# One or two products of the next weight job are put behind TensorE's own last work of five stages

## The chip, the cores and the metric

The kernel runs on one core of a Trainium2 chip. The metric is device time in microseconds (us) of one execution, lower is better. TensorE multiplies, ScalarE evaluates activations and copies, VectorE does elementwise work, GpSimd helps with memsets, some products and the gathers of cache pages, and SyncE issues most transfers.

## The reference

Two layers of a hybrid decoder trunk are computed for a prompt group (512 tokens) and a sample group (8 sequences of 4 tokens). A layer projects the normed input with one wide matrix, runs four mixers side by side, gates and sums their projected outputs, and ends with a gated feed-forward:

```python
h = rmsnorm(x, lp['norm1'])
(a_q, a_k, a_v, a_iq, a_ik, a_iw, r_q, r_k, r_v, r_g,
 c_q, c_f, c_i, c_g, m_z, m_xbc, m_dt, gates) = jnp.split(h @ lp['w_in'], SPLIT_POINTS, axis=-1)
...
o_a = attention_prompt(q, iq, iw, k, v, a_ik)          # A: top-k sparse attention
o_b, ret_new = retention_mixer(r_q, r_k, r_v, r_g, pos, states[0])     # B: retention
o_c, hgrn_new = hgrn2_mixer(c_q, c_f, c_i, c_g, lp['lb'], lp['hgrn_norm'], states[1])  # C: HGRN2
o_d, ssm_new, conv_new = mamba2_mixer(m_z, m_xbc, m_dt, ...)           # D: Mamba-2 with a causal conv
branches = jnp.stack([o_a, o_b, o_c, o_d], axis=2)
up = jnp.einsum('btnw,nwd->btnd', branches, lp['w_branch'])
g = jax.nn.sigmoid(gates.reshape(B, T, N_BRANCH, D_MODEL))
x = x + jnp.sum(g * up, axis=2) @ lp['w_out']
ff_gate, ff_up = jnp.split(rmsnorm(x, lp['norm2']) @ lp['w_gu'], 2, axis=-1)
x = x + (jax.nn.silu(ff_gate) * ff_up) @ lp['w_down']
```

All is float32. Both groups share the weights, so their 544 token columns go through every projection together.

## The kernel before

**Jobs and products.** The weights of a layer stream through two slots of the buffer `ring`, one job (512 columns of a weight matrix) in each. The jobs are `aq`, `akv`, `iq`, `ikiw`, `r0` to `r2`, `c2`, `r3`, `c0`, `c3`, `z`, `c1`, `xbc0`, `xbc1`, `dt`, then the gates and the branch projections in the order `gate00`, `gate01`, `wb00`, `gate10`, `wb01`, `gate11`, `wb10`, `gate20`, `wb11`, `gate21`, `wb20`, `gate30`, `wb21`, `gate31`, `wb30`, `wb31`, and last the jobs of the feed-forward. A job up to `wb31` is cut into products, the rows of the list `table`: a "natural" job has five (four token tiles of 128 and one of 32, at lines 369 and 372), a gate, `iq`, `c0` or `xbc` job eight (four strips of 128 output columns by two halves of 272 tokens, line 378), each of 8 matmuls, and a `wb` job eight of 4 matmuls. One matmul of a full product is called a unit here; the trace shows every float32 matmul as two records. `wb01#7` is the seventh product of `wb01`.

**Banks.** A product adds up in a bank of PSUM, `bank_of[k]`, mostly 6 or 7, in some stages one of three. Before its first matmul TensorE waits until the bank's last user has been read. Products of gate and projection jobs are read by ScalarE (`take_act`: a copy or an activation, and for the projections a transfer to DRAM), those of `wb` jobs by VectorE (`take_dve`: two instructions, lines 488 and 490, or one, line 485). The last product of a gate job is released only after a sigmoid over the whole gate. The first product of a gate job also waits in ScalarE's queue until VectorE has read the last `wb` product that used the same gate buffer.

**Stages and points.** The mixers run stage by stage, each written by hand for all engines: the end of stage A's projections (share `r0`), prompt attention (`c2`), sample attention (`dt`), retention (`wb01`), HGRN2 (`wb11`), the causal conv (`wb20`), the state space part (`gate31`), then the feed-forward. Between the mixer's own instructions stand points, at which a class `Share` fills products in: it spreads the units from where the last share ended to the end of the job it is named after over the points by a list of weights, so `Share("wb20", [4] + [1] * 8)` does four twelfths of its units at the first point. TensorE's `point` issues units up to its place, and the takers' `point` at the same index reads the products up to the one before the product that is under way there (`fill_to`):

```python
k = max(i for i in range(len(table)) if starts[i] < max(upto, 1))
take_to(who, eng, k - 1)
```

`share.end` finishes the job on each engine.

**Joins.** Each stage is a block that all five engines enter and leave together. Some stages are also a `part` of their own, behind which SyncE clears the stage's semaphores in a further block: so behind `wb01` and `wb11`, but not behind `r0`, `c2` and `wb20`. TensorE can't start the next stage before the last engine has left the one before.

In the conv stage TensorE first fills in products (the point with the weight 4), then turns the conv state (line 2055), ScalarE copies that (line 2029), and only then VectorE starts its convolutions (from line 2001), a sequence that goes on to the end of the stage, with `wb20`'s products read in between. Behind `share.end` TensorE makes short sums and transposes (lines 2064 to 2072) and ScalarE copies them out (lines 2046 and 2047). The top-k searches of the attention are long sequences on VectorE (lines 949 and 950), and the weights 1, 18, 25, 34 in the share `c2` are the units put beside them.

Of the kernel before, what the change touches and what calls it, by code (L numbers as in the profile page):

```python
# [133 lines left out]
def trunk(nc, inp, out):  # L134

    es = ExitStack()
    with es:
# [68 lines left out]
        class Arena:  # L206
            def __init__(self, t, at=0, end=None):
                self.t, self.at, self.end = t, at, end
# [103 lines left out]
        END = {}  # L312
# [14 lines left out]
            spare[name] = (2, 6, 7)  # L327
        bank_of, bank_before, last_use = [], [], [-1] * 8
        for k, row in enumerate(table):
            b = min(spare.get(row[0], (6, 7)), key=lambda i: last_use[i])  # L330
            bank_of.append(b)
            bank_before.append(last_use[b])
            last_use[b] = k
        starts = [0]
# [161 lines left out]
        def fill_to(who, eng, upto):  # L496

            if who == "pe":
                for x in range(done["pe"], upto):
                    k = max(i for i in range(len(table)) if starts[i] <= x)  # L500
                    product(eng, k, x - starts[k])
                done["pe"] = max(done["pe"], upto)
                return
            k = max(i for i in range(len(table)) if starts[i] < max(upto, 1))
            take_to(who, eng, k - 1)

        def take_to(who, eng, upto):
            for k in range(done[who], upto):
                if who == "act" and table[k][0][:4] == "gate" and table[k][5] == "act":

                    last = [i for i in range(k) if table[i][5] == "dve" and
                            table[i][0][3:] == table[k][0][5:]]
                    if last:
                        eng.wait_ge(S("taken_dve"), taken_by(last[-1])[1])
                (take_act if who == "act" else take_dve)(eng, k)
            done[who] = max(done[who], upto)

        def finish_to(who, eng, name):

            if who == "pe":  # L520
                fill_to("pe", eng, starts[END[name]])
            else:
                take_to(who, eng, END[name])

        class Share:

            def __init__(self, last, weights):
                self.a = {w: starts_at[0] for w in ("pe", "act", "dve")}
                self.a0, self.b = starts_at[0], starts[END[last]]
                self.cum = np.cumsum(weights) / np.sum(weights)  # L530
                self.p = {"pe": 0, "act": 0, "dve": 0}
                self.last = last
                starts_at[0] = self.b

            def point(self, who, eng):
                x = self.a0 + int(round((self.b - self.a0) * self.cum[self.p[who]]))
# [3 lines left out]
            def end(self, who, eng):  # L540
                assert self.p[who] in (0, len(self.cum)) or who == "dve", (who, self.p[who], len(self.cum))
                finish_to(who, eng, self.last)
        starts_at = [0]


# [116 lines left out]
        def stage_a(l):  # L662
# [48 lines left out]
            done["dve"] = END["ikiw"]  # L711
            starts_at[0] = starts[END["ikiw"]]

            share = Share("r0", [6, 12] + [1.2] * 10)
            with nc.Block() as block:
                @block.vector
                def _(dve):
# [83 lines left out]
            weights = []  # L801
            for i in range(NT):
                weights += [1] * 8 + [(1, 18, 25, 34)[i]] + [1] * 18
            share = Share("c2", weights)
            with nc.Block() as block:
                @block.sync
                def _(sp):
# [468 lines left out]
        def stage_retention(l):  # L1276
# [17 lines left out]
            qm = brT_[:, 8 * T + 2048:8 * T + 3072].rearrange("p (b n) -> p b n", b=NB)  # L1294
            kds = kT[:, P:2 * P]
            added = (0, 1, 4, 3)
            share = Share("wb01", [6] + [1] * 25)
            job0 = J["wb01"] - 1
            with nc.Block() as block:
                @block.tensor  # L1300
# [209 lines left out]
        def stage_hgrn(l):  # L1510
# [39 lines left out]
            zsum = cst[:, C["tri"][0]:C["tri"][0] + 1024]  # L1550
            lvz = K("lv_sum").rearrange("p (l t) -> p l t", l=7)
            mask = K("lv_mask").rearrange("p (s n) -> p s n", s=6)
            share = Share("wb11", [5] + [3, 3, 4, 4, 4, 3] * 4 + [3, 3, 4, 4, 4])
            with nc.Block() as block:
                @block.gpsimd
                def _(pool):
# [412 lines left out]
        def stage_ssm(l):  # L1969
# [14 lines left out]
            acc, accs = ar.take(2, SEQ), cv.take(2, NS)  # L1984
            ut, au = ar.take(5, 8), ar.take(5, 8)
            ea = ar.take(8)
            share = Share("wb20", [4] + [1] * 8)

            with nc.Block() as block:
                @block.gpsimd  # L1990
# [730 lines left out]
```

## Time and profile before

| | |
|---|---|
| times of three runs | 3776.77, 3788.73, 3782.89 us; median 3782.89 |
| profiled execution | 3787.7 us, its span in the trace 3785.9 |
| busy in the span | TensorE 91%, VectorE 46%, ScalarE 20%, GpSimd 7% |
| mean granted TensorE clock | 0.94 |
| moved | 366.11 MB in 274973 packets |

Times in the trace count from the start of the span. PE is TensorE, PEld its weight loads, DVE VectorE, ACT ScalarE, POOL GpSimd, SP SyncE; a q behind a name is the engine's sequencer. "Idle before" is time in which an engine had nothing to do, and what ended it is its releaser. A granted clock of 1.00 is 2.4 GHz, 0.50 is 1.2 GHz. The second layer repeats the first some 1857 us later with nearly the same rows.

### The profile page before, as it was taken

How to read it: one execution, taken by the hardware profiler on the slowest of the kernel's cores; microseconds unless marked ns; L12 is line 12 of the kernel's file. 1: busy time of each engine (PE TensorE's matmuls, PEld its weight loads, DVE VectorE, ACT ScalarE, POOL GpSimd, SP SyncE). 2: the span in 40 equal slices, each digit the busy share in tenths (PEclk: the TensorE clock that was granted, in tenths of full speed). 3: DMA queues.
4: the chain of work that ended last, by engine and by line, in shares of the span. 5: the costliest groups of instructions: out<-in, count | busy, mean ns of one | idle time of the engine just before them, and what ended most of it. 6: DMA issues, size and time to landing. Idle time of an engine off the chain costs nothing. (4 is left out here: it accounts for less than half of the span.)

```text
span 3785.9 us, 45247 instructions
## 1 busy us (share of the span) xinstructions
PE 3434.0 (91%) x18070; PEld 2409.5 (64%) x18070; DVE 1754.9 (46%) x3303; ACT 739.8 (20%) x1576; POOL 265.7 (7%) x266
## 2 busy tenths in 40 slices
PE   4988899989988989999989888999989998899998
PEld 2643454667666767888846434555776676678887
DVE  2135378114545445454512562951345454554543
ACT  1122222212322211010002222221123232110000
POOL 0000221210100010000000004112001000000000
PEclk8988899979999999999999889998899999999999
DMA  3221254452313221222232103555232231322221
GB/s 122 74 77 38 71 177 158 153 172 95 101 52 127 68 93 59 75 90 72 73 96 95 40 35 125 178 171 180 94 127 81 67 109 37 115 67 89 67 81 66
DMA packets 274973, 366.11 MB, mean 97 GB/s; under 512 B 39262, under 2 KB 171230, under 8 KB 274628
## 3 DMA queue, kind: packets, MB, share of 16 engines
q1 hardware_dynamic: 232348, 260.85, 21.1%
q0 software_dynamic: 21504, 75.51, 6.1%
q10 hardware_dynamic: 20904, 26.78, 2.0%
q8 instruction: 146, 2.39, 0.3%
q14 instruction: 71, 0.58, 0.0%
HBM read 312.76 MB, written 50.34 MB: 96 GB/s over the span
## 5 line engine op out<-in xcount | busy, mean ns | idle before, releaser
L378 PE MATMUL ps<-hT,ring 128*128 128x272 f32 x3072 | 780.6, 409 | 61.8 <-PEq L155 32.3
L378 PEld LDWEIGHTS ps<-hT,ring 128*128 128x128 f32 x3072 | 593.1, 198 | 213.7 <-issue 56.5
L372 PE MATMUL ps<-ring,hT 128*128 128x512 f32 (+3 forms) x1600 | 661.0, 555 | 34.5 <-DVE hT L625 18.3
L372 PEld LDWEIGHTS ps<-ring,hT 128*128 128x128 f32 (+1 forms) x1600 | 280.3, 199 | 327.1 <-issue 302.9
L378 PE MATMUL ps<-branchT,ring 128*128 128x272 f32 x1024 | 264.2, 412 | 38.5 <-DVE arena L488 23.7
L2511 PE MATMUL ps<-hT,ring 128*128 128x272 f32 x1136 | 279.0, 396 | 17.4 <-DVE hT L2636 17.4
L378 PEld LDWEIGHTS ps<-branchT,ring 128*128 128x128 f32 x1024 | 198.4, 198 | 97.0 <-DVE arena L488 28.6
L2511 PEld LDWEIGHTS ps<-hT,ring 128*128 128x128 f32 x1136 | 217.9, 192 | 63.6 <-issue 18.2
L2511 PE MATMUL ps<-arena,ring 128*128 128x272 f32 x720 | 177.9, 401 | 13.3 <-PEq L155 10.6
L2511 PEld LDWEIGHTS ps<-arena,ring 128*128 128x128 f32 x720 | 139.8, 195 | 44.5 <-issue 11.4
L949 DVE MAX8 branchT<-arena 32x8 f32<-32x2080 f32 x64 | 148.2, 2316 | 2.2
L950 DVE MATCH_REPLACE8 arena<-branchT,arena 32x2080 f32<-32x2080 f32 x64 | 147.0, 2296 | 0.0
L2522 ACT ACTIVATE arena<-ps 128x272 f32<-128x272 f32 x68 | 27.1, 398 | 519.7 <-PE ps L2511 519.7
L2511 PE MATMUL ps<-branchT,ring 128*128 128x272 f32 x512 | 127.1, 392 | 0.0
L2511 PE MATMUL ps<-branchT,arena 128*128 128x272 f32 x448 | 111.1, 392 | 0.0
L2511 PEld LDWEIGHTS ps<-branchT,ring 128*128 128x128 f32 x512 | 97.3, 190 | 20.1
L1188 ACT ACTIVATE branchT<-ps 128x512 f32<-128x512 f32 x128 | 69.5, 594 | 194.7 <-PE ps L1093 194.4
L721 DVE TENSOR_TENSOR branchT<-arena 128x2560 f32<-128x2560 f32 (+1 forms) x4 | 8.6, 2154 | 190.6 <-PEq L681 190.6
L2511 PEld LDWEIGHTS ps<-branchT,arena 128*128 128x128 f32 x448 | 85.1, 190 | 17.5
L2511 PE MATMUL ps<-branchT,stage 128*128 128x272 f32 x352 | 87.8, 392 | 0.0
L840 PE MATMUL ps<-cst,arena 128*128 128x128 f32 x160 | 35.4, 327 | 52.0 <-ACT arena L891 51.7
L1267 DVE TENSOR_SCALAR rows_at<-rows_at 128x32 int32<-128x32 int32 x2 | 0.4, 180 | 168.2 <-PE ps L1157 168.2
(481 smaller groups left out, 4473.4 us busy)
## 6 DMA issues: line engine op xcount, KB each, us to landing
ring<-in_w_in SPq DMA_DIRECT2D x44, 2048.0 KB, 8.1
ring<-in_w_gu SPq DMA_DIRECT2D x44, 1024.0 KB, 6.5
spill<-stage ACTq DMA_DIRECT2D x72, 256.0 KB
arena<-spill SPq DMA_DIRECT2D x16, 1024.0 KB, 5.9
ring<-in_w_branch SPq DMA_DIRECT2D x16, 1024.0 KB, 5.1
ring<-in_w_down SPq DMA_DIRECT2D x8, 1536.0 KB, 6.6
ring<-in_w_down SPq DMA_DIRECT2D x8, 1280.0 KB, 5.9
ring<-in_w_out SPq DMA_DIRECT2D x4, 2048.0 KB, 9.2
```

The source lines that it names most:

```text
L372: mm = pe.matmul(bank[0:m, 0:w], hT[:, c, t0:t0 + m], slot3(j)[:, c, 0:w], start=(c == 0), stop=(c == kn - 1))
L378: mm = pe.matmul(bank[:, 0:HALF], slot3(j)[:, c, at:at + P], src, start=(c == 0), stop=(c == kn - 1))
L721: vch.link(dve, dve.tensor_tensor(t2, a2, a2, ALU.mult))
L840: mm = pe.transpose(ps[2 + n % 2][:, s * P:s * P + P], Pr[:, n % 2, s * P:s * P + P], ident)
L949: vch.link(dve, dve.max(m, src))
L950: vch.link(dve, dve.match_replace(work, m, src, TAKEN))
L1188: act.activation(KT[:, bb, j, :], ps[j][:, :], ACT.Copy).then_inc(S("kt_ready"), 1)
L1267: vch.link(dve, dve.tensor_scalar(rows_at[:, :], rows_at[:, :], float(n_rows // DEPTH), None, ALU.add))
L2511: mm = pe.matmul(bank(n, p), left[:, c, :], r[:, c, :], start=(c == 0), stop=(c == k - 1))
L2522: act.activation(part_of[n % 2][0], bank(n, 1), ACT.Copy).then_inc(S("p1_copied"), 1)
```

## The change

A `Share` gets a third argument, `more`. Its points are spread as before up to the end of the job it is named after, but on all engines `share.end` then goes on for `more` products of the next job, and the next share starts behind these. It is 1 for `r0` (first product of `r1`) and `c2` (first of `r3`), and 2 for `wb01` (`gate11`), `wb11` (`gate21`) and `wb20` (`gate30`). The first two products of these gates are kept to banks 6 and 7.

```diff
+            early = row[0] in ("gate11", "gate21", "gate30") and row[2] == 0
-            b = min(spare.get(row[0], (6, 7)), key=lambda i: last_use[i])
+            b = min((6, 7) if early else spare.get(row[0], (6, 7)), key=lambda i: last_use[i])
...
-            def __init__(self, last, weights):
-                self.a = {w: starts_at[0] for w in ("pe", "act", "dve")}
-                self.a0, self.b = starts_at[0], starts[END[last]]
+            def __init__(self, last, weights, more=0):
+
+                self.a0, self.b, self.upto = starts_at[0], starts[END[last]], END[last] + more
...
-                starts_at[0] = self.b
+                starts_at[0] = starts[self.upto]
...
             def end(self, who, eng):
...
                 finish_to(who, eng, self.last)
+                if who == "pe":
+                    fill_to("pe", eng, starts[self.upto])
+                else:
+                    take_to(who, eng, self.upto)
...
-            share = Share("r0", [6, 12] + [1.2] * 10)
+            share = Share("r0", [6, 12] + [1.2] * 10, 1)
...
-            share = Share("c2", weights)
+            share = Share("c2", weights, 1)
...
-            share = Share("wb01", [6] + [1] * 25)
+            share = Share("wb01", [6] + [1] * 25, 2)
...
-            share = Share("wb11", [5] + [3, 3, 4, 4, 4, 3] * 4 + [3, 3, 4, 4, 4])
+            share = Share("wb11", [5] + [3, 3, 4, 4, 4, 3] * 4 + [3, 3, 4, 4, 4], 2)
...
-            share = Share("wb20", [4] + [1] * 8)
+            share = Share("wb20", [4] + [1] * 8, 2)
```

The lines below the class stand five further down in the changed kernel, so line 378 is 379 there, and line 2055 is 2060. On TensorE the end of the retention stage and the start of the HGRN2 stage (the branches are the join) read so before; `ring` stands for the streamed weights:

```order
L1360 MATMUL ps<-branchT 128x512 x4
L378 MATMUL ps<-branchT,ring 128x272 x8
L1360 MATMUL ps<-branchT 128x512 x4
L1299 UNCONDITIONAL_BRANCH
L1573 UNCONDITIONAL_BRANCH
L378 MATMUL ps<-hT,ring 128x272 x9
L1580 MATMUL ps<-cst,arena 128x128 x4
L1585 MATMUL ps<-arena,cst 128x512
```

and so with the change:

```order
L1365 MATMUL ps<-branchT 128x512 x4
L379 MATMUL ps<-branchT,ring 128x272 x8
L1365 MATMUL ps<-branchT 128x512 x4
L379 MATMUL ps<-hT,ring 128x272 x16
L1304 UNCONDITIONAL_BRANCH
L1578 UNCONDITIONAL_BRANCH
L379 MATMUL ps<-hT,ring 128x272 x8
L1585 MATMUL ps<-cst,arena 128x128 x4
L1590 MATMUL ps<-arena,cst 128x512
```

Sixteen matmuls of `gate11` stand ahead of the join, and the first point behind it has 8 in place of 9. On TensorE the conv stage reads so before (from its first row to the start of the sums behind `share.end`):

```order
L378 MATMUL ps<-hT,ring 128x272 x32
L2055 MATMUL ps<-cst,branchT 128x24 x8
L378 MATMUL ps<-hT,ring 128x272 x32
L378 MATMUL ps<-branchT,ring 128x272 x32
L2064 MATMUL ps<-arena,cst 128x8 x12
```

and so with the change:

```order
L379 MATMUL ps<-hT,ring 128x272 x27
L2060 MATMUL ps<-cst,branchT 128x24 x8
L379 MATMUL ps<-hT,ring 128x272 x21
L379 MATMUL ps<-branchT,ring 128x272 x32
L379 MATMUL ps<-hT,ring 128x272 x16
L2069 MATMUL ps<-arena,cst 128x8 x12
```

Ahead of the conv state's transposes stand 27 matmuls in place of 32, behind them 21 in place of 32, and 16 of `gate30` come in between `wb20` and the sums.

## Rows read from the trace of the kernel before

**Rows 1.** The page: busy us of the engines, with share and instructions.
```profile
PE 3434.0 (91%) x18070; PEld 2409.5 (64%) x18070; DVE 1754.9 (46%) x3303; ACT 739.8 (20%) x1576; POOL 265.7 (7%) x266
```

**Rows 2.** Windows a:b, shares c2, dt, wb11, wb20, gate31: length, busy by engine, clock.
```profile
206.85:430.48 223.63, 190.62 (x768) 92.10 (x769) 121.61 (x320) 55.05 (x147) 0.04 (x1) 0.85 0.14 49
430.48:813.38 382.90, 354.75 (x1983) 206.28 (x1983) 176.77 (x159) 88.41 (x180) 98.36 (x98) 0.91 0.49 164
...
975.78:1165.41 189.63, 169.53 (x1618) 119.09 (x1619) 96.68 (x268) 56.51 (x101) 21.10 (x20) 0.94 0.23 72
1165.41:1229.42 64.01, 54.64 (x244) 43.87 (x245) 35.73 (x87) 20.43 (x46) 0.00 (x0) 0.93 0.45 141
1229.42:1411.16 181.74, 160.14 (x822) 126.60 (x823) 86.25 (x142) 35.75 (x71) 11.26 (x8) 0.95 0.23 72
```

**Rows 3.** Timeline at the joins behind r0 and c2: start, us, engine, line.
```profile
205.25 1.10 ACTq L463 DMA_DIRECT2D spill<-stage  x1
206.85 0.46 PE L822 MATMUL ps<-arena 64*128 64x128 f32 x2 [2.54 <-PEq L715]
...
427.79 0.59 ACT L445 ACTIVATE stage<-ps 128x512 f32<-128x512 f32 x1
428.41 0.33 ACTq L463 DMA_DIRECT2D spill<-stage  x1
...
429.14 0.53 ACTq L463 DMA_DIRECT2D spill<-stage  x1
...
430.48 0.99 PE L1040 MATMUL ps<-arena,cst 32*128 32x8 f32 x4 [3.22 <-PEq L805]
```

**Rows 4.** Timeline at the joins behind wb01, wb11 and wb20.
```profile
972.97 0.78 DVE L485 TENSOR_TENSOR arena<-ps,xT 128x272 f32<-128x272 f32 x2
...
975.78 6.24 PE L378 MATMUL ps<-hT,ring 128*128 128x272 f32 x18 [5.22 <-PEq L155]
...
1161.98 0.44 DVE L490 TENSOR_TENSOR arena<-arena 128x272 f32<-128x272 f32 x1
...
1165.41 17.53 PE L378 MATMUL ps<-hT,ring 128*128 128x272 f32 x64 [4.00 <-PEq L155]
...
1229.42 1.09 PE L2160 MATMUL ps<-cst,arena 128*128 128x128 f32 x4 [3.50 <-PEq L1989]
```

**Rows 5.** Timeline: two runs of products without a wait.
```profile
368.27 20.01 PE L372 MATMUL ps<-ring,hT 128*128 128x512 f32 x46
...
1191.47 12.81 PE L378 MATMUL ps<-hT,ring 128*128 128x272 f32 x48 [4.07 <-ACT xT L416]
```

**Rows 6.** TensorE's waits: who, for whom: us in total, times, longest.
```profile
PE ps L840 <- ACT arena L891: 51.7, 10, 9.4
...
PE ps L378 <- DVE arena L488: 29.8, 14, 4.3
...
PE ps L2230 <- DVE arena L2367: 16.2, 6, 6.1
```

**Rows 7.** Timeline of the conv stage: its first step and its end.
```profile
1184.39 0.29 DVE L2001 COPY arena<-arena 128x256 f32<-128x256 f32 x1 [21.97 <-ACT arena L2029]
...
1219.20 2.10 PE L378 MATMUL ps<-branchT,ring 128*128 128x272 f32 x8 [0.60 <-DVE arena L488]
...
1221.13 2.74 PE L2064 MATMUL ps<-arena,cst 128*128 128x8 f32 x24
...
1222.03 0.44 DVE L490 TENSOR_TENSOR arena<-arena 128x272 f32<-128x272 f32 x1
```

**Rows 8.** Timeline and windows: a short wait, and the clock behind waits.
```profile
1046.65 2.85 PE L378 MATMUL ps<-branchT,ring 128*128 128x272 f32 x8 [2.03 <-ACT xT L419]
...
975.78:979.60 3.82, 3.82 (x9) 2.89 (x10) 3.58 (x3) 1.24 (x1) 3.27 (x3) 0.50 1.03 290
1047.80:1051.30 3.50, 3.50 (x8) 2.02 (x7) 2.63 (x8) 0.69 (x3) 0.00 (x0) 0.51 0.15 33
1165.41:1170.70 5.29, 5.29 (x12) 4.02 (x13) 0.00 (x0) 0.00 (x0) 0.00 (x0) 0.50 0.93 286
```

## The prediction

> **What bounds the kernel now.** I read the page first: TensorE is busy 91% of the span, VectorE 46% [rows 1]. The windows by stage say the same of each stage the change touches: in the prompt attention (`c2`) TensorE is busy 190.6 of 223.6 us against VectorE's 121.6, in HGRN2 (`wb11`) 169.5 of 189.6 against 96.7, in the conv stage (`wb20`) 54.6 of 64.0 against 35.7 [rows 2]. So a stage mostly lasts as long as TensorE's own program, and the change leaves that program's instructions alone; it moves some across five joins. Two questions remain. How much of the idle time at a join do the moved products use up? And does the next stage get shorter by all that it has lost? The timeline at the joins answers the first: TensorE stands 2.54, 3.22, 5.22, 4.00 and 3.50 us [rows 3, 4], 18.5 us in a layer, 37 us in both. The list of TensorE's waits answers the second: it also waits inside stages, for the top-k searches 51.7 us (line 840, mostly one wait in each of three query blocks), for VectorE to read `wb` products 29.8 us (line 378), and in the state space stage 16.2 us (line 2230) [rows 6]. A unit taken away in front of such a wait only makes it longer.
>
> **What a moved product costs.** 46 records of natural products took 20.01 us, 48 of gate products 12.81 us less their tail, about 0.435 and 0.235 to 0.267 a record [rows 5]. A product has 16 records: I take 7.0 us for a natural one and 3.75 us for a gate's at full speed, so 7.5 us for two. A natural unit is then 0.87 us, a gate's 0.47 us. Each layer moves 7.0, 7.0, 7.5, 7.5 and 7.5 us.
>
> **The joins and the stages behind them, one layer.** Each time: what the join comes later, then what the next stage gives back.
>
> Behind `r0`. The 2.54 us are ScalarE's: it reads the last product and issues its transfer from 205.25 to 206.35, and TensorE goes on at 206.85 [rows 3]. With `r1#1` behind it, the same follows the new last product; its bank is free, so TensorE runs on for 7.0 us. Only the transfer is shorter (that of a full tile is issued in 0.33 us, row 428.41, not in 1.10), so the join is +6.2 us. Next, share `c2` has 112 units in place of 120, by weights that sum to 182, of which 78 lie at the searches. There the stage goes by VectorE, and 3.4 of the 8 units come off the long waits [rows 6]; the other 4.6 units give 4.0 us. Together +2.2.
>
> Behind `c2`. ScalarE reads the last products of the old job only from 427.79 on [rows 3], and `r3#1` needs the bank of the first of them, so it starts 1.1 us late and ends at 435.4. Reading it (0.6) and issuing the transfer (0.33) take 1.1 with what lies between them, and leaving the block 0.8, as from 429.67 to 430.48 [rows 3]: the join comes at 437.3 in place of 430.48, +6.8. The sample attention has TensorE busy 354.8 of 382.9 us [rows 2] and gives back 8 units, 6.8 with a little lost at its gathers. Together 0.
>
> Behind `wb01`. Here VectorE is last. It ends at 973.75, TensorE at 970.56, and TensorE starts again 2.0 us after VectorE (two blocks, with the semaphores cleared between) [rows 4]. The two `gate11` products run 970.56 to 978.1; their banks are free, the second's at 973.4 when it is wanted at 974.3. ScalarE reads the last until 978.6, plus 2.0: 980.65 against 975.78, +4.9. This join hides 2.6 us. HGRN2 gives back 16 units, 7.5, less what goes into waits. One unit at its first point is lost, since TensorE waits there for VectorE's first sequence anyway, and the waits for VectorE at `wb` products eat more. Against that the products shift along the points: `wb10`, which was spread over two token tiles, falls into one, and the read of its last product, for which `gate20` waited, comes a point earlier, ahead of a long VectorE sequence; the sigmoid of `gate11` comes two points earlier, ahead of copies that TensorE needs. I take −6.1. Together −1.2.
>
> Behind `wb11`. VectorE ends at 1162.42, TensorE at 1161.41, and TensorE restarts 3.0 later [rows 4]. The two `gate21` products end at 1168.9, their read at 1169.4, the restart is at 1172.4: +7.0, so this join hides half a microsecond. The conv stage gives back little. Its length is TensorE's first point (17.53 us [rows 4]) and then VectorE's own sequence from 1184.39 to 1222.47, 38.1 us, for which TensorE waits, not the reverse: `wb20#8` starts at 1219.20, when VectorE has read `wb20#5` [rows 7]. So of 16 units only those at the first point count, 5 (27 for 32), 2.3 us. Together +4.7.
>
> Behind `wb20`. The two `gate30` products stand ahead of the sums of line 2064, which now start at 1221.13, and for which ScalarE's copies and then the join wait [rows 7]. The first needs the bank of `wb20#6`, read 2.4 us before VectorE's end (the reads follow each other at 0.95 us: `wb20#5` at 1219.15, `wb20#8` by 1222.47 [rows 7]), the second that of `wb20#8`. So they run from 2.4 us before VectorE's end to 5.1 after it, where the sums now start 1.3 before it: +6.5. The state space stage gives back 16 units, 7.5, less some 2.5 units in front of the wait of line 2230 [rows 6], plus about 1.3 us since the 4.3 us wait for VectorE meets TensorE later: −7.3. Together −0.8.
>
> The sum is 2.2 + 0 − 1.2 + 4.7 − 0.8 = +4.9 us a layer.
>
> **The clock.** Behind the `wb01` join TensorE works 3.82 us at a granted 0.50, behind `wb11` 5.29 us [rows 8], which costs 1.9 and 2.6 us. With the change the first gap shrinks from 5.22 to about 2.5. A wait of only 2.03 us was followed by 3.50 us at 0.51 [rows 8], so the half clock does not go away; I take back 1.0 us a layer, with 0 and 4.5 as ends. The Trainium skill (TensorE: Matmul & The Clock Gate, Why this matters for your kernels) advises keeping idle gaps between bursts of matmuls short, so that the clock stays up; by it the `wb01` join would be spared its half clock, 1.9 us a layer. The trace speaks against it at gaps of this length, with the 2.03 us wait.
>
> **Forecast.** 4.9 − 1.0 = +3.9 us a layer, +7.8 in all. Against the profiled execution's own 3787.7 us that is 3795.5; that execution lies 4.8 above the median, so the median becomes about **3791**, or +0.2%. Within 0.3%, 11.3 us here, a measurement of this kernel can't tell it from no change.
>
> **Ends of the terms.** The joins' +6.2, 6.8, 4.9, 7.0, 6.5 are sure to about 0.5 each. What is not known is what HGRN2 and the state space stage give back. Above, each can't give more than 7.5 plus its waits for VectorE's reads; I take 10. Below, all units could land in front of waits; I take 3. The searches could take all 8 units' worth of waiting and the clock with it: 3 us more.
>
> **Rivals.**
> *Slower: HGRN2 and the state space stage give back half.* Place: TensorE at `wb` products, where it waits for VectorE's point. VectorE gets there after a fixed sequence of its own from something TensorE made, so a thinner filling reaches the bank sooner and waits longer. For it: the fourteen waits of line 378 [rows 6]. Against it: VectorE is busy only 96.7 of 189.6 us there [rows 2]. It gives 6.7 in place of 13.4 a layer: +10.6 a layer, 3804. It decides from 1.7 us a layer missing, where the whole passes 0.3%.
> *The conv stage follows TensorE after all.* Then it gives back 7.5, not 2.3: −1.3 a layer, 3780. For it: TensorE is busy 54.6 of 64.0 us [rows 2]. Against it: VectorE's unbroken sequence behind 1184.39.
> *The clock stays up behind the joins* (the rule above). Both 1.9 and 2.6 are spared, 3.5 a layer more than I took: +0.4 a layer, 3784. The 2.03 us wait speaks against it [rows 8]. With the rival before it, −4.8 a layer: 3773, at the edge of faster.
> That the change does not do what it says is out: the order has 16 more matmuls ahead of the join.
>
> **Chances.** Forecast 0.45 (3780 to 3798), slower rival 0.30, conv rival 0.10, clock rival 0.10, both 0.05. Of the forecast's 0.45 a fifth lies past +0.3%; of the slower rival nine tenths do; of the two single ones a fifth lies past −0.3%. With half of the double one and 0.02 for what I have missed, faster is 0.04 + 0.03 + 0.02 = 0.09, slower 0.09 + 0.27 = 0.36, and same 0.55. The range reaches from the double rival to the slower one: 3774 to 3804.
>
> **What would show it.** In the profile after: gaps at the joins of about 2.3, 3.3 (in two parts), 2.5, 3.5 and 3.5 us; the conv stage's VectorE sequence still 38 us, and the stage from its first product to the next stage's first longer than 64.0 us, about 68; HGRN2 from join to join 189.6 − 6.1 + 7.0, about 190.5; the top-k waits longer by 0.7 to 1.3 us each. I am wrong if HGRN2 or the state space stage differ by over 3 us from this, or if VectorE's sequence in the conv stage stretches or shrinks. The feed-forward, 497.8 us a layer, must not change.

## The result, and the profile after

The changed kernel takes 3798.47 us (median of 11 runs) against 3785.64 for the kernel before (11 runs): ratio 1.0038, 95% interval 1.0027 to 1.0048, so +14 us and slower by a little more than the measurement's uncertainty. I had forecast 3791, in a range of 3774 to 3804, with most of the chance on "no difference". One of the 11 runs, at 4449 us, was disturbed and is left out of the ratio; the median of the other ten is 3795.6.

The profiled execution took 3792.77 us (span 3791.0), only 5 above that of before. That is chance, since layer 1 of before held the longer form of a stage that varies by itself, as the windows show. First the page's busy row, which answers to [rows 1]: TensorE did the same 18070 matmuls in 11.0 us less.

```profile
PE 3423.0 (90%) x18070; PEld 2407.1 (63%) x18070; DVE 1755.6 (46%) x3303; ACT 739.6 (20%) x1576; POOL 264.2 (7%) x266
```

Then the windows of after, from each join to the next, as in [rows 2]: shares c2, dt, wb11, wb20 and gate31 of layer 1, and behind the "..." the same five of layer 2.

```profile
211.94:432.52 220.58, 183.16 (x768) 91.11 (x769) 121.66 (x320) 55.87 (x148) 0.04 (x1) 0.86 0.15 54
432.52:803.56 371.04, 342.71 (x1967) 200.93 (x1967) 176.90 (x159) 86.53 (x178) 98.00 (x98) 0.93 0.49 166
969.13:1155.78 186.65, 166.44 (x1618) 117.47 (x1619) 96.09 (x268) 56.55 (x101) 21.34 (x19) 0.95 0.21 68
1155.78:1222.90 67.12, 54.33 (x244) 42.63 (x245) 35.72 (x87) 20.64 (x46) 0.12 (x2) 0.95 0.41 131
1222.90:1404.42 181.52, 157.00 (x790) 123.19 (x791) 86.46 (x141) 35.07 (x69) 11.27 (x8) 0.92 0.23 72
...
2075.35:2299.54 224.19, 186.76 (x769) 92.49 (x769) 121.69 (x320) 55.88 (x148) 0.04 (x1) 0.85 0.15 53
2299.54:2670.63 371.09, 342.81 (x1967) 200.91 (x1967) 176.95 (x159) 86.54 (x178) 97.92 (x98) 0.93 0.49 166
2836.13:3022.70 186.57, 165.76 (x1618) 117.29 (x1619) 96.70 (x268) 56.55 (x101) 21.39 (x19) 0.96 0.22 68
3022.70:3091.93 69.23, 56.38 (x245) 43.59 (x245) 35.73 (x88) 20.66 (x46) 0.12 (x2) 0.89 0.40 127
3091.93:3272.84 180.91, 156.27 (x790) 122.73 (x791) 86.33 (x141) 35.06 (x69) 11.27 (x8) 0.92 0.23 72
```

What to compare them with needs care, because a stage with an unchanged program doesn't always last as long. [rows 2] shows layer 1 of before. The windows of its layer 2 (same shares, same columns) are:

```profile
2074.64:2290.97 216.33, 183.30 (x769) 89.14 (x769) 121.61 (x320) 54.95 (x147) 0.04 (x1) 0.90 0.14 50
2290.97:2673.67 382.70, 354.76 (x1982) 206.30 (x1983) 176.83 (x159) 88.40 (x180) 98.23 (x98) 0.91 0.49 164
2834.28:3022.39 188.11, 169.66 (x1618) 119.31 (x1619) 96.43 (x268) 56.51 (x101) 22.43 (x20) 0.94 0.23 73
3022.39:3086.33 63.94, 54.54 (x244) 43.73 (x245) 35.71 (x87) 20.43 (x46) 0.00 (x0) 0.93 0.44 141
3086.33:3268.51 182.18, 160.57 (x823) 126.94 (x823) 86.24 (x142) 35.75 (x71) 11.26 (x8) 0.95 0.23 72
```

The prompt attention took 223.6 us in layer 1 and 216.3 in layer 2, with the same instructions and the same VectorE time; TensorE's busy time is 190.6 against 183.3, and its clock 0.85 against 0.90. Of the 14 such stages in the seven profiles here that don't touch it, nine lasted 216.2 to 218.3 us and five 221.5 to 223.7 (mean of all 218.9). HGRN2 varies too where nothing near it was changed: 188.1 us in seven of the 14 such stages, 189.6 to 192.2 in the other seven. The other stages of layer 2 are what most profiles repeat to some tenths, so layer 2 of before is my base below; for these two stages a difference of a few us says little. By stage, from the first TensorE instruction behind a join to the first behind the next (us, after less base):

| stage | base | after, layer 1 / 2 | difference | predicted |
|---|---|---|---|---|
| r0 | 39.6 | 45.8 / 45.8 | +6.2 / +6.2 | +6.2 |
| prompt attention (c2) | 216.3 (mean 218.9) | 220.6 / 224.2 | +4.3 / +7.9 | +2.8 |
| sample attention (dt) | 382.7 | 371.0 / 371.1 | −11.7 / −11.6 | −6.8 |
| wb01 | 160.6 | 165.6 / 165.5 | +5.0 / +4.9 | +4.9 |
| HGRN2 (wb11) | 188.1 | 186.7 / 186.6 | −1.5 / −1.5 | +0.9 |
| conv (wb20) | 63.9 | 67.1 / 69.2 | +3.2 / +5.3 | +4.2 |
| state space (gate31) | 182.2 | 181.5 / 180.9 | −0.7 / −1.3 | −7.3 |
| sum | | | +4.8 / +9.9 | +4.9 |

The sum of the joins and stages came to +4.8 and +9.9 us a layer, 15 in all, like the ratio's 14. Layer 1's is what I had summed before the clock was taken off, but two of its terms are off by 5 to 7 us in opposite directions.

The timeline at the join behind r0 and at the one behind wb01, after, to set beside [rows 3, 4]:

```profile
203.34 7.13 PE L373 MATMUL ps<-ring,hT 128*128 128x512 f32 x16
...
210.52 0.60 ACT L446 ACTIVATE stage<-ps 128x512 f32<-128x512 f32 x1 [6.19 <-PE ps L373]
...
211.94 0.46 PE L827 MATMUL ps<-arena 64*128 64x128 f32 x2 [1.46 <-PEq L720]
...
969.13 3.90 PE L379 MATMUL ps<-hT,ring 128*128 128x272 f32 x16 [2.36 <-PEq L155]
...
976.65 0.70 PE L1590 MATMUL ps<-arena,cst 128*128 128x512 f32 x1 [3.17 <-DVE arena L1823]
```

The joins did what the prediction's steps say: product, ScalarE's read, the short transfer (none behind `wb01`), restart. The gaps are 1.5, 1.5, 2.4, 3.1 and 3.5 us. The first is shorter than the 2.3 I had said; by my own +6.2 for a product of 7.0 us it should have been 1.7. The second, with a wait of 1.27 us just before the moved product, makes 2.7 in two parts for 3.3. The last row is a wait that was not among those of before: HGRN2's own product of line 1590 stands 3.17 us for VectorE. And behind the `wb01` join, where [rows 8] has 3.82 us at a granted 0.50, the clock is now at full:

```profile
969.13:972.95 3.82, 3.82 (x17) 3.14 (x18) 3.42 (x3) 1.28 (x1) 3.42 (x3) 1.00 0.96 279
```

### The profile page after: what moved, and what is told of

Same layout as the page of the kernel before. It is cut to its first block and busy times, and to the rows that moved or that the text cites. A ratio compares the mean times of both kernels' runs of the same rounds, so it can differ in the third digit from the quotient of the medians.

```text
span 3791.0 us, 45251 instructions
## 1 busy us (share of the span) xinstructions
PE 3423.0 (90%) x18070; PEld 2407.1 (63%) x18070; DVE 1755.6 (46%) x3303; ACT 739.6 (20%) x1576; POOL 264.2 (7%) x266
## 5 line engine op out<-in xcount | busy, mean ns | idle before, releaser
L379 PEld LDWEIGHTS ps<-hT,ring 128*128 128x128 f32 x3072 | 583.6, 195 | 199.4 <-issue 55.8
L373 PE MATMUL ps<-ring,hT 128*128 128x512 f32 (+3 forms) x1600 | 649.5, 548 | 34.2 <-DVE hT L630 18.7
L2516 PEld LDWEIGHTS ps<-hT,ring 128*128 128x128 f32 x1136 | 218.8, 193 | 64.0 <-issue 18.2
L1193 ACT ACTIVATE branchT<-ps 128x512 f32<-128x512 f32 x128 | 69.5, 594 | 189.8 <-PE ps L1098 188.8
L726 DVE TENSOR_TENSOR branchT<-arena 128x2560 f32<-128x2560 f32 (+1 forms) x4 | 8.6, 2156 | 190.3 <-PEq L686 190.3
L896 ACT ACTIVATE arena<-arena 128x128 f32<-128x128 f32 (+3 forms) x64 | 36.0, 562 | 223.1 <-DVE arena L937 222.1
L845 PE MATMUL ps<-cst,arena 128*128 128x128 f32 x160 | 37.8, 347 | 45.8 <-ACT arena L896 45.8
```

The costliest lines, as they stand in the source:

```text
L373: mm = pe.matmul(bank[0:m, 0:w], hT[:, c, t0:t0 + m], slot3(j)[:, c, 0:w], start=(c == 0), stop=(c == kn - 1))
L379: mm = pe.matmul(bank[:, 0:HALF], slot3(j)[:, c, at:at + P], src, start=(c == 0), stop=(c == kn - 1))
L726: vch.link(dve, dve.tensor_tensor(t2, a2, a2, ALU.mult))
L845: mm = pe.transpose(ps[2 + n % 2][:, s * P:s * P + P], Pr[:, n % 2, s * P:s * P + P], ident)
L896: act.activation(Pr[:, n % 2, 0:L], St[:, n % 2, 0:L], ACT.Exp, bias=mx[:, n % 2, 0:1], accum_out=sm[:, n % 2, 0:1]).then_inc(S("att_probs ...
L1193: act.activation(KT[:, bb, j, :], ps[j][:, :], ACT.Copy).then_inc(S("kt_ready"), 1)
```

## The experiments

Ratios are to runs of the kernel before on the same chip; us in brackets are the ratio less one, times 3783.

### Each join alone

In each of these five runs one Share keeps its last argument and the other four have 0 in its place (and only the row of its own products is `early`). For r0:

```diff
-            share = Share("c2", weights, 1)
+            share = Share("c2", weights, 0)
-            share = Share("wb01", [6] + [1] * 25, 2)
+            share = Share("wb01", [6] + [1] * 25, 0)
...
```

**r0 alone.** 

> Only the first of the five joins is moved: one product behind r0, so r0 is longer by 6.1 us a layer, as in the full change, and the prompt attention has 112 units in place of 120. By the prediction the prompt attention gives back 4.0 us (219.6 us in layer 1, 212.3 in layer 2), since 3.4 of the 8 units lie in front of the top-k waits: +2.1 us a layer, +4 in all. By the rival (the searches take all 8 units) it gives back under 1 us: +10 in all. By a third reading the clock decides: then the prompt attention's change has another sign in one layer than in the other, and goes with the length of its half-clock stretches.

Measured: 1.0022, interval 1.0010 to 1.0033 (+8 us, 4 to 12). r0 45.83; the prompt attention 217.6 and 220.0 us, where the mean of the unchanged ones is 218.9: nothing given back in these two stages, with 69 and 72 us at half clock. Against the same layers of before that is −6.0 and +3.7, so the signs differ as in the third reading, but half clock went from 68.7 to 69.1 us in layer 1 and from 45.0 to 72.1 in layer 2: it explains layer 2 and not layer 1. In the full change, the same stage less its own join's 6.5 us is 214.1 and 217.7, 3 us below the mean. The interval of the ratio just reaches my +4, and the stage's own spread is as large as the question. So the time leans to the rival and does not decide; TensorE's waits, further down, lie between the two readings.

**Behind the prompt attention alone.** 

> Only the join behind the prompt attention is moved: that stage +6.8 us, the sample attention -6.8 by the prediction, 0 in all. By the rival reading of the full change's trace, in which the sample attention fell by 11.9 and 11.6 us, it falls by about 11.7 here too, because a stretch of half clock goes away with the join's gap: -5 us a layer, -10 in all. If the 5 us beyond the product's 7 belong to the other moves, the sample attention shows -7 here.

Measured: 0.9985, 0.9973 to 0.9997 (−6 us). The stage is 222.8 in layer 2, +6.5 (229.5 in layer 1, +5.9 over that layer's long form). The sample attention falls to 372.7 and 371.4, so −10.0 and −11.3: the move's own doing, by the second expectation. There TensorE's busy time fell by 9.8 and 11.8, though one product is 7.0. Some 3 us of the rest are alike in both layers. Before, two waits in the stage were each followed by 3.41 us at half clock with TensorE busy throughout. With the move both waits are shorter (0.91 us became 0.57, 2.27 became 1.72) and no half clock follows. The second of them, before and with the move:

```profile
640.56 7.11 PE L372 MATMUL ps<-ring,hT 128*128 128x512 f32 x12 [2.27 <-ACT stage L458]
...
641.66:645.08 3.42, 3.42 (x6) 1.36 (x5) 3.35 (x4) 0.00 (x0) 0.00 (x0) 0.50 0.48 186
```
```profile
656.05 1.52 PE L370 MATMUL ps<-ring,hT 128*32 128x128 f32 x48 [1.72 <-ACT stage L459]
...
653.90:660.70 6.80, 3.85 (x77) 2.97 (x76) 1.60 (x3) 4.13 (x8) 2.11 (x2) 1.00 0.56 144
```

In layer 2 the last stretch at half clock changed too. First before, then with this join moved:

```profile
2638.50:2679.40 40.90, 32.76 (x172) 22.15 (x172) 1.69 (x9) 2.81 (x8) 4.00 (x4) 0.50 0.57 202
```
```profile
2628.40:2648.80 20.40, 20.11 (x130) 11.27 (x131) 0.00 (x0) 0.90 (x4) 4.81 (x5) 0.50 0.64 243
...
2652.20:2665.90 13.70, 6.79 (x24) 5.86 (x24) 1.69 (x9) 1.28 (x1) 0.00 (x0) 0.50 0.52 183
```

There one stretch of 40.9 us became 20.4 and 13.7, and in the whole stage half clock fell from 65.3 to 54.4 us. Before, a wait of 0.72 us for a gathered cache page ends 0.9 us ahead of the stretch; with the move the clock falls during one of 0.77 us. But such waits are not what brings it. In layer 1 the same place has no wait over 0.5 us with the move, TensorE is busy for all of the 6.9 us before, with short matmuls (8 columns, or 256 against weights of 32 columns), and the clock falls all the same, for 41.0 us:

```profile
764.60:771.50 6.90, 6.90 (x73) 4.29 (x76) 0.00 (x0) 0.85 (x3) 4.01 (x4) 1.00 0.82 286
771.50:812.50 41.00, 33.62 (x187) 22.12 (x188) 1.69 (x9) 2.81 (x8) 6.01 (x6) 0.50 0.56 204
```

So layer 1 gives back its 10 us (7.0 and twice 1.7) without this last part, and why the stretch breaks in layer 2 is open.

**Behind wb01 alone.** 

> Only the join behind wb01 is moved, two gate11 products: wb01 +4.9 us, HGRN2 -6.1 by the prediction, -1.2 a layer, -2 in all. By the sizes read from the full change's trace wb01 is +3.2 to +4.9 and HGRN2, with nothing added at its own end, -10.0 to -8.5: -5 a layer, -10 in all. By the slower rival HGRN2 gives back about 3 us only: +2 a layer, +4 in all.

Measured: 0.9986, 0.9977 to 0.9996 (−5 us). wb01 165.1 in layer 2 (+4.5), HGRN2 180.6 and 182.1 (−7.5 and −6.0), the conv stage behind it +0.8 and +1.0. The size of my −6.1 holds and the slower rival falls: HGRN2 does not give back half. In layer 1 it is made up otherwise than I had it: TensorE's waits inside the stage are 3.5 us longer (one of 3.4 us at line 1590 is new), and half clock fell from 24.3 to 14.2 us.

**Behind HGRN2 alone.** 

> Only the join behind HGRN2 is moved: HGRN2 +7.0 us, the conv stage -2.3 by the prediction since from its first point on VectorE's own sequence of 38 us sets its end, so +4.7 a layer, +9 in all. By the rival (the conv stage follows TensorE) the conv stage gives back 7.5: -0.5 a layer, -1 in all. VectorE's sequence in the conv stage stays 38 us by the first and shrinks by about 5 by the second.

Measured: 0.9999, 0.9990 to 1.0009. HGRN2 +6.5 in layer 1 (+8.1 in layer 2), the conv stage −7.5. The rival's length, but not by its cause. The conv stage, and its first 5.29 us, where [rows 8] has a clock of 0.50:

```profile
1160.85:1217.29 56.44, 46.35 (x212) 36.47 (x213) 35.70 (x88) 19.85 (x44) 0.12 (x2) 0.94 0.49 155
1160.85:1166.14 5.29, 5.29 (x23) 4.43 (x24) 0.00 (x0) 0.40 (x1) 0.12 (x2) 1.00 0.77 239
```

And the timeline of VectorE's sequence there, first row and last:

```profile
1174.91 0.29 DVE L2006 COPY arena<-arena 128x256 f32<-128x256 f32 x1 [23.47 <-ACT arena L2034]
...
1212.53 0.44 DVE L491 TENSOR_TENSOR arena<-arena 128x272 f32<-128x272 f32 x1
```

VectorE's sequence lasts 38.06 us, from 1174.91 to 1212.97; before it was 38.08 [rows 7]. So the stage is fixed by VectorE, as I said. But it starts 14.06 us behind the join instead of 18.98: 2.3 for the five units and 2.6 because the join is followed by no half clock. And TensorE ends 0.8 us behind VectorE (at 1213.80, the 3.49 us gap before 1217.29) instead of 3.5: with fewer units at every point its last `wb20` product stands earlier in VectorE's sequence, so that VectorE has three products left to read behind its last own step instead of four, and the sums of line 2069 run beside that. 2.3 + 2.6 + 2.6 = 7.5.

**Behind the conv stage alone.** 

> Only the join behind the conv stage is moved, two gate30 products: the conv stage +6.5 us, and by the prediction the state space stage -7.3, so -0.8 a layer, -2 in all. By the theory drawn from the full change's trace the state space stage gives back only 0.2 to 1.3 us, because TensorE's waits there for VectorE get longer (by 2.9) and each is followed by more half clock: +5.8 a layer, +12 in all. If the state space stage falls by over 5 us here, its failure in the full change came from the moves before it, not from its own.

Measured: 1.0049, 1.0034 to 1.0065 (+19 us, 13 to 25). The conv stage 72.2 and 71.7, +8.3 and +7.8, where I had 6.5. The `gate30` products can't start 2.4 us before VectorE's end, since TensorE is still at `wb20#8`: they start 1.3 before it, and the sums 6.0 after it. Also, TensorE's clock falls during the short matmuls behind them, and half clock in the stage goes from 9.3 to 14.2 us in layer 1 (10.3 in layer 2). The state space stage is 182.0 and 181.3: it gives back nothing to 0.9. Only this move and r0's lose more than the measurement's uncertainty, and this one more clearly. The ratios of the five single moves sum to +8 −6 −5 0 +19 = +16 us; the full change is +14.

### Moves together

Arguments 0, 1, 2, 0, 0 for the first, 0, 1, 2, 2, 0 for the second.

> The two joins whose moves gained alone, behind the prompt attention and behind wb01. If the joins' parts add up: -6.3 and -5.0 us, -11.3 in all, ratio 0.9970; sample attention -11.4 and HGRN2 -7 a layer. Rival (the moves eat each other's gain, since the products' order shifts for every later stage): over -6 in all.

Measured: 0.9962, 0.9949 to 0.9974 (−14 us; the parts give −11). The sample attention is 372.8 and 371.0, HGRN2 183.6 and 180.2 (−4.5 and −7.9). This is the lowest ratio here, though the intervals of the next kernel and of the last one below overlap it.

> As the kernel with two joins, and the one behind HGRN2 too, which alone measured 0.0. Adding: -11.3 us in all; HGRN2 -7 +6.4, the conv stage -7.5 to 56.5 us with no half clock behind its join. Rival: the two moves on either side of HGRN2 leave its share with the new wait that the full change shows at its start (3.17 us), HGRN2 is 3 us longer than the parts add up to, and the kernel is slower than the one with two joins by 6 us or more.

Measured: 0.9976, 0.9967 to 0.9985 (−9 us, parts −11). The sample attention is 375.5 in layer 1, with 65.1 us at half clock, and 371.0 in layer 2, with 54.0. HGRN2 186.4 and 190.3, conv 58.1 and 58.0, against 56.4 alone: behind this join the clock is at half again for 3.1 to 3.3 us. The interval overlaps that of the kernel with two; that the third move costs 5 us is not shown.

### The prompt attention's points

```diff
-                weights += [1] * 8 + [(1, 18, 25, 34)[i]] + [1] * 18
+                weights += [1] * 8 + [(1, 20, 30, 38)[i]] + [1] * 18
```

> The join behind r0 alone, as measured before at +11.2 us, and the points of the prompt attention weighted so that the three long searches have 12, 17 and 22 units of filling as in the kernel before, where the move alone leaves 11, 15 and 21; the missing units come off the other points. By the theory that the thinner filling of the searches (longer wait, and a longer half clock behind it: 61 us of it in place of 48) ate the 7 us, the prompt attention falls by 5 to 7 us from 216.5, r0 stays +6.1, and the kernel is within 3 us of before. By the rival (the units at the other points don't count, TensorE is not what they wait for) it stays at 217.6 to 220, +11 in all.

Measured: 1.0014, 1.0005 to 1.0023 (+5 us, 2 to 9); the stage 219.3 and 213.1. The two ratios overlap. The expectation failed where it counts: TensorE's waits inside the stage are 29.7 us before, 34.6 with r0 moved and 34.5 with the weights too. The first long search of layer 2, before, with r0 moved, and with the weights:

```profile
2110.95 8.85 PE L372 MATMUL ps<-ring,hT 128*128 128x512 f32 x20
...
2130.95 0.66 PE L840 MATMUL ps<-cst,arena 128*128 128x128 f32 x2 [9.36 <-ACT arena L891]
```
```profile
2113.64 1.95 PE L370 MATMUL ps<-ring,hT 128*32 128x128 f32 x64
...
2130.35 0.66 PE L845 MATMUL ps<-cst,arena 128*128 128x128 f32 x2 [13.07 <-ACT arena L896]
```
```profile
2117.83 1.95 PE L370 MATMUL ps<-ring,hT 128*32 128x128 f32 x64
...
2133.68 0.66 PE L845 MATMUL ps<-cst,arena 128*128 128x128 f32 x2 [13.27 <-ACT arena L896]
```

A unit is not always the same time. A product of the 32-token tile counts eight units like one of 128 tokens (each is four short matmuls there), but takes 1.95 us and not 7.0. With one product moved, the whole of such a product (64 records) falls beside the first search, with only 8 records of 0.43 us, where before there were 20 of them and half of a small product. So TensorE is through 4.2 us earlier and waits 13.1 us in place of 9.4. The weights gave units back, but not time. The other two long waits are 8.8 us in place of 8.5 (now for a bank that ScalarE reads behind the search) and 8.3 in place of 7.3. Together the waits eat 4.9 of the product's 7 us; what is left of it is less than half clock moves in this stage, with 69 and 72 us of it here. A split by time instead of units was not tried.

### Why the state space stage gives nothing back

Waits of TensorE in this stage of layer 1, before and with only the gate30 products moved:

```profile
PE ps L2230 <- DVE arena L2367: 8.1, 3, 6.1
PE ps L378 <- DVE arena L488: 5.1, 2, 4.3
```
```profile
PE ps L2235 <- DVE arena L2372: 12.0, 4, 7.0
PE ps L379 <- DVE arena L489: 3.3, 2, 2.4
PE ps L379 <- ACT arena L420: 2.7, 1, 2.7
```

All its waits behind the join come to 16.2 us before and 19.0 with the move (nine waits in either, of which four and then five are over 1 us). TensorE's busy time is 160.1 and 157.7: 2.5 less, for 32 records of 0.235 us, 7.5 less. The other 5 us are half clock, 17.9 us of it before, 28.5 now (18.3 and 27.7 in layer 2).

My first theory was that the stage's length is a chain of hand-overs, and that filling doesn't matter. Two gate30 products computed twice (same result) should then cost nothing:

```diff
+                if k in (END["gate30"] - 6, END["gate30"] - 5):
+                    for x in (2 * c % 8, 2 * c % 8 + 1):
+                        mm = pe.matmul(bank[:, 0:HALF], slot3(j)[:, x, at:at + P], hT[:, x, half * HALF:half * HALF + HALF],
+                                       start=(x == 0), stop=(x == 7))
```

> As the kernel with two gate30 products moved behind the conv stage alone, and two later gate30 products are computed twice, which gives TensorE back the 16 units (7.5 us) of filling that the state space stage had lost; the result is the same. By the theory that this stage's length is set by what VectorE, ScalarE and TensorE hand each other, and that filling goes into TensorE's waits and into time at half clock, the stage stays at 182 us (181.3 to 183), its time at half clock falls from 28 to about 18 us and TensorE's waits by 2 to 3. By the rival (TensorE sets the stage) it grows by 7.5 to 189.5. The conv stage stays 72.

Measured: 1.0067, 1.0053 to 1.0081 (+25 us). The stage grew to 189.8 and 187.7, by 7.7 and 6.4, with the same waits as before the addition (12.0 us at line 2240, 3.3 at line 384 for VectorE, and 2.7 for ScalarE, all in layer 1). So the theory fell as I had put it: filling does matter. But the doubled products stand at the stage's first points, ahead of its first wait, so the run shows only that work put there costs its full time; it does not test filling in front of a wait. (The kernel's +25 is 6 above the +19 of the move alone, less than the 14 of the two stages; the intervals, 20 to 31 and 13 to 25, are too wide to tell.) What remains is where the units stand. Next, the points of this stage weighted so that those ahead of the line 2235 wait keep their units:

```diff
-            share = Share("gate31", [1, 4] + [2, 2, 2, 2, 1] * 5)
+            share = Share("gate31", [1, 4] + [2, 2, 2.4, 2.4, 1] * 5)
```

> As the kernel with two gate30 products moved behind the conv stage alone, with the state space stage's points weighted so that the two points ahead of each wait for the output rows (the third and fourth of a token tile) hold 6.4 units as in the kernel before, where the move alone leaves 5.8; the missing units come off the two points before them. Two products computed twice left every wait and the time at half clock as they were and cost their full 6.2 to 7.5 us, so the stage is not of fixed length: what ate the 7.5 us is that the waits got longer where the filling thinned, and a half clock behind each. By that the stage falls from 181.3 to 182.0 to 175 to 178 us, with 18 us at half clock in place of 28. By the rival (the handing over between the engines takes its time wherever the units stand) new waits open at the thinned points and it stays at 181 to 182.

Measured: 1.0025, 1.0014 to 1.0036 (+9 us, where the move alone had +19). The window of this stage in layer 1, with the move alone (181.25 us in layer 2), then with the weights (176.63):

```profile
1226.15:1408.16 182.01, 157.66 (x790) 123.81 (x791) 86.40 (x142) 35.05 (x69) 11.27 (x8) 0.92 0.23 72
```
```profile
1235.94:1412.44 176.50, 152.76 (x791) 120.37 (x791) 86.32 (x142) 35.06 (x69) 11.26 (x8) 0.94 0.24 74
```

The stage fell by 5.5 and 4.6, into the expected range. Of layer 1's 5.5, 4.9 are TensorE's busy time, for the same 790 matmuls: the clock (half clock 28.5 to 19.5 us). Its waits came to 18.5 us in place of 19.0, and there are nine of them in either, so neither their sum nor their number makes the difference. In layer 1 it lies behind two single waits. With the move alone the first of these is followed by 3.41 us at half clock and the second by 6.8:

```profile
1271.43 5.16 PE L379 MATMUL ps<-branchT,ring 128*128 128x272 f32 x14 [2.75 <-ACT arena L420]
...
1325.10 0.66 PE L2235 MATMUL ps<-cst,arena 128*128 128x128 f32 x4 [2.45 <-DVE arena L2372]
...
1326.40:1333.20 6.80, 6.11 (x31) 4.50 (x30) 1.61 (x3) 1.70 (x5) 0.00 (x0) 0.50 0.01 4
```

Before, the same two waits were 1.74 and 1.61 us, and with the weights they are 1.83 and 1.54; no half clock follows them there, in either layer:

```profile
1279.33 2.10 PE L379 MATMUL ps<-branchT,ring 128*128 128x272 f32 x8 [1.83 <-ACT arena L420]
...
1331.90 0.66 PE L2235 MATMUL ps<-cst,arena 128*128 128x128 f32 x4 [1.54 <-DVE arena L2372]
```

In layer 2 with the move alone the second wait (2.46 us) was not followed by half clock, but a later stretch was longer (10.2 us for 6.8), so the wait's length is not all that decides.

> The kernel before with those weights of the state space stage and no product moved: the control for the run with the same weights. If the weights only restore what the move had thinned, this stage stays within 1.5 us of 182.0 and the kernel within 3 us of before. If the weights are a gain of their own, it falls by as much here.

Measured: 0.9987, 0.9974 to 1.0000 (−5 us). The stage is 180.1 and 178.5, so the weights gain 2.1 and 3.7 us by themselves: neither "under 1.5" nor "as much". With these weights the two moved products give back 3.6 and 1.9 us, without them 0.2 and 0.9.

### A join the change left alone

```diff
-            share = Share("dt", [1.2] * 16 + [2.6] * 32 + [6, 8] + [4] + [1] * 16 + [3] + [1] * 16)
+            share = Share("dt", [1.2] * 16 + [2.6] * 32 + [6, 8] + [4] + [1] * 16 + [3] + [1] * 16, 2)
```

> The two joins that gained together (behind the prompt attention and behind wb01), and a join that the change left alone: two gate00 products behind the sample attention, where TensorE stands 6.91 us. The gap hides most of their 7.5 us, so the sample attention is longer by 1 to 2.5 us (371 to 373), and the wb01 stage, which has 16 units less, falls from 165.7 by 3 to 7: -2 to -5 a layer beyond the kernel with the two joins, ratio to before about 0.994. By the rival (what a stage loses goes into its waits and half clock, as in the state space stage) the wb01 stage falls by under 1.5 and the kernel is no faster than that one, 0.996.

Measured: 0.9969, 0.9957 to 0.9982 (−12 us; the two joins alone −14). The sample attention came to 379.1 in layer 2, +8.0 over 371.0, since the gap shrank only from 6.91 to 5.34:

```profile
809.14 0.40 ACT L417 ACTIVATE arena<-ps 128x272 f32<-128x272 f32 x1 [3.27 <-PE ps L379]
814.44 0.79 PE L379 MATMUL ps<-hT,ring 128*128 128x272 f32 x1 [5.34 <-PEq L155]
```

The wb01 stage gave back 8.6 (157.1 for 165.7). Both sizes lie outside what I expected (+1 to 2.5, and −3 to −7), and together they come to nothing. A gap hides a product only if it does not start after the product: this one is 5 us of leaving one block and entering the next behind the last engine. What fills those 5 us I did not test.

## Why the prediction was right and wrong

**The joins' lateness** was right: +6.2 (measured +6.2), +6.8 (+6.5), +4.9 (+4.4 to 5.1, once 6.3), +7.0 (+6.5), and +6.5 behind the conv stage. Alone, that one cost +8.3 and 7.8, with 0.8 for the later start of its products and the rest half clock. In the full change it came out as written. There the earlier move takes `wb20`'s last product out of the way, and the first `gate30` product waits for VectorE's read of its bank:

```profile
1171.36 0.29 DVE L2006 COPY arena<-arena 128x256 f32<-128x256 f32 x1 [24.99 <-ACT arena L2034]
...
1207.20 7.57 PE L379 MATMUL ps<-hT,ring 128*128 128x272 f32 x32 [1.57 <-DVE arena L489]
...
1208.99 0.44 DVE L491 TENSOR_TENSOR arena<-arena 128x272 f32<-128x272 f32 x1
...
1214.61 2.74 PE L2069 MATMUL ps<-arena,cst 128*128 128x8 f32 x24
```

VectorE's sequence lasts 38.07 us and ends at 1209.43. The products start 2.2 us before that end and the sums 5.2 after it, where I had 2.4 and 5.1.

**"3.4 of the 8 units come off the long waits; the other 4.6 units give 4.0 us"**, in the prompt attention, was mis-sized, since it took every natural unit for 0.87 us. The long waits grew by 3.7, 0.3 and 1.1 us and all waits by 4.9, where the forecast had 0.7 to 1.3 each. In the full change the stage gave back 2.2 us in layer 1 and was 1.4 longer in layer 2; how much of that is the move and how much the stage's own spread, these profiles can't tell.

**"The sample attention gives back 8 units, 6.8 with a little lost"**: the size was off: 10.0 and 11.3 alone, 11.7 and 11.6 in the full change (7.2 in one layer of the kernel with three moves). About 3 us more are the two short stretches of half clock that went with their shorter waits; the rest goes with the last stretch, 41 us in some layers and broken in others.

**HGRN2, −6.1**: right in size, −6.0 and −7.5 alone, −4.5 and −7.9 in the kernel with two moves. That it holds in layer 1 too is partly luck: a new wait of 3.4 us at line 1590, where I had one unit lost, is paid for by less half clock.

**"The conv stage gives back little … 2.3 us"**: the mechanism, VectorE's 38 us, was right. In layer 1 of the full change its sequence starts 15.58 us behind the join for 18.98: 2.3 for the five units, as forecast, and 1.1 for a shorter half clock (3.1 us for 5.3). So the stage came to +3.1 where I had +4.2; in layer 2 half clock in the short matmuls at its end adds 2.1. The 7.5 of the move alone holds 1.5 us more of clock at the start, and 2.6 for one product fewer to read at the end, where in the full change the `gate30` products run. So the conv rival's stage gain was met alone, by another cause, and not in the full change.

**"The state space stage gives back 16 units, 7.5 … −7.3"** is the step that failed, 6 to 7 us a layer. It counted two and a half units in front of a wait and the rest as time saved (its own terms add to 7.6, not 7.3). The trace shows 7.5 us less work, 2.8 us more waiting, and 5 us lost to more half clock, in layer 1 behind two waits that had grown by about 1 us. That the places of the units do this, not their number, is shown by the weights: the same 16 units moved, and 5.5 and 4.6 us less. This is the slower rival's loss, in one of its two stages; the longer waits are its mechanism, the half clock is not.

**"I take back 1.0 us a layer" for the clock** was too low at the joins and had the wrong scope. At the `wb01` join the gap fell from 5.22 to 2.36 us, and the clock stayed at 1.00 where it had been at 0.50 for 3.82 us: 1.9 us, which I had argued away with the 2.03 us wait. So it went in nine of the ten layers with this move, in five kernels. Behind `wb11` half clock fell from 5.29 to 3.1 us, another 1.1. That is 3.0 us a layer, and much of HGRN2's −1.5 for +0.9. But half clock also moved inside stages, by 3 to 5 us in two of them, in both directions. The Trainium skill (TensorE: Matmul & The Clock Gate, Why this matters for your kernels) asks for short idle gaps. At the `wb01` join this held, against my reading. Behind `wb11`, after 3.09 us of idle, the clock stayed at 1.00 with this move alone, where it fell after 4.00. With all moves the same 3.09 us were followed by half clock again, so the length of the gap does not settle it:

```profile
1155.78:1158.90 3.12, 3.12 (x7) 2.42 (x8) 0.00 (x0) 0.00 (x0) 0.12 (x2) 0.51 0.59 143
```

**The level**: +3.9 a layer forecast, about +7 measured. The median came out 7 us above the 3791, or 5 by the 3795.6. It lies inside the range, but just past the forecast's own 3780 to 3798, on the side of the slower rival's 3804. That it is so near is partly luck, because the errors of a layer partly cancel: −4.9 in the sample attention and −2.4 in HGRN2 against +6.3 in the state space stage and +1.5 to +5.1 in the prompt attention. "Slower" had 0.36 in my list and "same" 0.55.

## What to carry to other kernels

When a change thins the filling that a scheduler spreads over a stage, cost it point by point, in time and not in units: units in front of a wait come back as waiting, and a wait that grows by 1 us can be followed by half clock that costs as much again. Move work across a join one join at a time; here two of five gain (0.9962 together), and one alone loses more than they bring. Before reading a stage's change off one pair of profiles, see how the same stage differs between the layers and between kernels that don't touch it.

## What the runs showed of the hardware

- The same program has two lengths in one stage: the prompt attention 216 or 223 us, with 45 to 53 us at half clock or 60 to 69, in layer 1 or 2 alike. HGRN2 has 188.1 us or 189.6 to 192.2. What decides it stays open.
- Half clock (a granted 0.50, 1.2 GHz of 2.4) came without any wait, behind 6.9 us in which TensorE was busy throughout with short matmuls, and lasted 41.0 us with TensorE busy for 33.6 of them (layer 1, prompt attention's join moved).
- Waits of like length can be followed by half clock or not: 2.27 us by 3.4 us of it and 1.72 by none (sample attention), 2.45 by 6.8 us and 1.54 by none (state space stage), but 3.09 behind the `wb11` join by none in one kernel and by 3.1 us in another.
- Nor does the wait fix how long it lasts. With r0's join moved, an 8.8 us wait in the prompt attention goes with 34.1 us at half clock, of which TensorE is busy for 29.7; before, the wait at the same search (8.5 us) went with 6.8 us.
